# Low parts of the weights at another address remainder: residue 64 instead of 128 modulo 256

## The reference

```python
x = x + 0.5 * swiglu(rms_norm(x, ffn1_norm), w_gate, w_up, w_down)   # (silu(h @ w_gate) * (h @ w_up)) @ w_down
h = rms_norm(x, mix_norm)
z, xbc, dt, u = split(h @ w_in)
y_ssd  = ssd_group(z, xbc, dt, ...)        # conv, chunked scan over 16 heads, gate, grouped norm
y_pool = multiscale_pool_group(u, ...)     # trailing means over 2/4/8/16, a linear map per group
x = x + concat(y_ssd, y_pool) @ w_out
x = x + 0.5 * swiglu(rms_norm(x, ffn2_norm), w_gate2, w_up2, w_down2)
out = rms_norm(x, final_norm)
```

## The kernel before

| tensor | residue |
|---|---|
| `w_hi_part` (address 1152), `w_lo_part` (address 17536) | 128 |
| `xT`, `xghi`, `xglo` (lower four tiles of the normed input) | 128 |
| `xumhi`, `xumlo` (its upper four tiles in the mixer), `mixhi`, `mixlo`, `acthi`, `actlo` | 128 |
| `xufhi`, `xuflo` (its upper four tiles in the feed-forward blocks), `thi`, `tlo`, `post`, `gbuf` | 64 |

## Time and profile before

### The profile page before, as it was taken

The page is one execution under the profiler, slowest core; times in us unless marked ns, Lnnn a source line. Parts: engine busy times, 40 slices in busy tenths (PEclk is TensorE's granted clock), DMA queues, the critical chain, the costliest instruction groups (busy, mean ns, idle before and its releaser), DMA issues.

```text
span 999.2 us, 15359 instructions
## 1 busy us (share of the span) xinstructions
PE 984.2 (99%) x6118; PEld 867.7 (87%) x6118; DVE 781.2 (78%) x983; ACT 464.0 (46%) x603; POOL 215.8 (22%) x179
## 2 busy tenths in 40 slices
PE   9999999999999999999999999999999999999996
PEld 7799889998999868878787878889988999889975
DVE  5888478985698798786799886798956899568964
ACT  6655235552355556552224653545522555225532
POOL 1012002310022352321063461201300123002321
PEclk9999999999999999999999999999999999999998
DMA  9526304452232333323222232353551345313302
GB/s 264 151 61 161 104 22 127 127 148 85 60 108 67 103 108 94 97 64 83 66 85 66 67 101 85 87 146 86 145 149 45 85 124 153 106 42 105 107 22 85
DMA packets 188655, 99.63 MB, mean 100 GB/s; under 512 B 3524, under 2 KB 187944, under 8 KB 188584
## 3 DMA queue, kind: packets, MB, share of 16 engines
q1 hardware_dynamic: 187912, 97.60, 35.4%
q10 hardware_dynamic: 672, 1.05, 0.3%
HBM read 96.54 MB, written 2.10 MB: 99 GB/s over the span
## 4 chain that ended last, share of the span: by engine, by line
PE 91%; DVE 6%; issue 1%; ACT 1%; POOL 0%; POOLq 0%; DVEq 0%; ACTq 0%
PE bank L1643 12%; PE bank L1641 12%; PE bank L1642 12%; PE bank L1576 9%; PE bank L1578 9%; PE bank L1577 9%; PE bank L1659 8%; PE bank L1660 7%; PE bank L1661 7%; DVE w_lo_part L998 1%; PE bank L1730 1%; DVE actlo L1026 1%; PE bank L1724 1%; PE bank L1727 1%; DVE upd L1129 1%
## 5 line engine op out<-in xcount | busy, mean ns | idle before, releaser
L566 POOL TENSOR_TENSOR post<-post,rstd 128x256 f32<-128x256 f32 x57 | 93.1, 1634 | 520.9 <-DVE post L1088 520.9
L1641 PE MATMUL bank<-thi,w_hi_part 128*128 128x256 f32 x608 | 168.0, 276 | 0.0
L1642 PE MATMUL bank<-tlo,w_hi_part 128*128 128x256 f32 x608 | 167.9, 276 | 0.0
L1643 PE MATMUL bank<-thi,w_lo_part 128*128 128x256 f32 x608 | 167.9, 276 | 0.0
L998 DVE TENSOR_TENSOR w_lo_part<-w_raw,w_hi_part 128x1024 fp32r<-128x1024 f32 (+1 forms) x102 | 130.6, 1281 | 16.7 <-ACT w_hi_part L663 14.5
L1659 PE MATMUL bank<-acthi,w_hi_part 128*128 128x512 f32 x346 | 135.6, 392 | 2.1 <-DVE actlo L1026 2.1
L1661 PE MATMUL bank<-acthi,w_lo_part 128*128 128x512 f32 x346 | 134.7, 389 | 0.0
L1660 PE MATMUL bank<-actlo,w_hi_part 128*128 128x512 f32 x346 | 134.7, 389 | 0.0
L1641 PEld LDWEIGHTS bank<-thi,w_hi_part 128*128 128x128 f32 x608 | 114.2, 188 | 0.0
L1642 PEld LDWEIGHTS bank<-tlo,w_hi_part 128*128 128x128 f32 x608 | 114.2, 188 | 0.0
L1643 PEld LDWEIGHTS bank<-thi,w_lo_part 128*128 128x128 f32 x608 | 114.2, 188 | 0.0
(11 more groups left out here) (295 smaller groups left out, 2315.8 us busy)
## 6 DMA issues: line engine op xcount, KB each, us to landing
w_raw<-in_ffn_w_gate SPq DMA_DIRECT2D x42, 512.0 KB, 4.0
w_raw<-in_ffn_w_up SPq DMA_DIRECT2D x42, 512.0 KB, 5.2
w_raw<-in_ffn_w_down SPq DMA_DIRECT2D x32, 512.0 KB, 5.1
w_raw<-in_w_in SPq DMA_DIRECT2D x29, 512.0 KB, 3.8
w_raw<-in_w_out SPq DMA_DIRECT2D x16, 512.0 KB, 3.9
w_raw<-in_ffn_w_down SPq DMA_DIRECT2D x16, 384.0 KB, 4.4
out<-xtok SPq DMA_DIRECT2D x4, 512.0 KB, 3.1
xload<-in_x SPq DMA_DIRECT2D x3, 512.0 KB, 7.2
```

Of the source, the lines that this page charges most:

```text
L566: pool.tensor_tensor(gate, gate, rstd[:, half(h)], ALU.mult).then_inc(ready, 1)
L1641: pe.matmul(out, w, hi, start=opens and e == 0 and k == 0, stop=False, skip_group_check=True)
L1642: pe.matmul(out, w, lo, start=False, stop=False, skip_group_check=True)
L1643: mm = pe.matmul(out, wl, hi, start=False, stop=end, skip_group_check=True)
```

## The change

`w_lo_part` is moved up by 192 bytes: three small tables of 64 bytes each (`fold`, `a_exp`, `skip_row`) are declared between the two rings, and a fourth (`inv_count`, 64 bytes) behind `w_lo_part`, so that the next large tensor `xT` is 256 bytes higher than before and keeps its residue. The address of `w_lo_part` is 17728, its residue 64; `w_hi_part` stays at 1152. The tensors from `xT` to `par` are 256 bytes higher; what lies above the small tables stays where it was. The instructions of all engines, their order, their waits and the transfers are the same as before; lines from L223 on have another number (from the middle of the declarations on, one more).

```diff
         whi = sb("w_hi_part", [P, RING, UB, P], F32R)
+        fold = sb("fold", [2 * LOW, HEADS])
+        a_exp = sb("a_exp", [P, HEADS])
+        skip_row = sb("skip_row", [P, HEADS])
         wlo = sb("w_lo_part", [P, RING, UB, P], F32R)
+        inv_count = sb("inv_count", [P, PAD])
+        assert nc.sbuf_base % LANES == WEIGHT_LANE
         xT = sb("xT", [P, DK * S])
...
         eps = sb("eps", [P, 1])
-        inv_count = sb("inv_count", [P, PAD])
         dt_bias = sb("dt_bias", [2 * LOW, 1])
-        fold = sb("fold", [2 * LOW, HEADS])
-        a_exp = sb("a_exp", [P, HEADS])
-        skip_row = sb("skip_row", [P, HEADS])
         skip_col = sb("skip_col", [P, DK])
```

## The result

The changed kernel takes 1018.13 us (1017.57 to 1018.70, 2 runs) against 1001.16 before: the ratio is 1.017, with a 95% interval of 1.0146 to 1.0195. The forecast was 1006.5, with a range up to 1018.0. The span grew from 999.2 to 1015.8 us, by 16.6.

The account below looks back on a forecast made before the run. TensorE's matmul pace, start to start, was taken as the bound. Terms 6.1 + 0 − 0.5 − 0.3 = +5.3 us on 1000.9 gave 1006.2, forecast as 1006.5 us after 0.3 to the median; range 994 to 1018.

Parts of the forecast that it names:

- rival 2: Alternating differences inside every triple slow TensorE, half to all of 25 us: 1014 to 1026, taken as 1019; chance 0.16.
- the additive reading: Forecast's basis: each matmul's pace follows its own load-to-moving residue difference, alternation costing 0; 1002 to 1011 us, chance 0.42.
- (a): Second matmuls, 256 columns, moving residue 64: 912 now at equal residues, 113.3 to 120.0 ns, +6.1 us.
- (b): Second matmuls, 512 columns, moving residue 128: 746 with load 64 below, an unseen difference; taken as 0, ±4.5 us.
- (e): Cost of the difference alternating inside every triple: 0 to 25 us, 0.02 us per 256-column triple; taken as 0.
- Both signs: Named as proving the forecast wrong: the triples' other two matmuls carry the change, or the 512-column stages do.
- (c): Second matmuls, 256 columns, moving residue 128 (xglo): 152, between 0 and −1.0 us, taken as −0.5.
- (d): Second matmuls, 512 columns, moving residue 64: 48 go from 233 to 227 ns, −0.3 us.
- (f): VectorE's write of w_lo at residue 64 costs nothing more, nor do the moved small tables: 0.
- Rival 1: Only the moving operand's own residue counts, so nothing changes: 1001.2 us within 1 us; chance 0.20.
- Rival 3: Load 64 below the moving operand is faster: sum −5.8 us, 995.4 us, or 990 with two steps; chance 0.22.

Follow-up runs that it names:

- e3: Kernel before with both weight rings at residue 64 in place of 128, moving operands as before; 1020.4 us.
- e10: Changed kernel with grouped order in each unit: high times high and high times low for all blocks, then low times high; 1016.18 us, ratio 1.0146.
- e12: Kernel before with the lower tiles of xg (xghi, xglo) at residue 64 in the feed-forward blocks; 1009.22 us, ratio 1.0078.
- e1: Kernel before with all four small tables between the weight rings, low parts 256 bytes higher, residue still 128; 1001.19 us, ratio 1.0001.
- e6: Kernel before with both weight rings at residue 192 in place of 128, moving operands as before; 1026.0 us.
- e7: Kernel before with only the low weight parts moved, to residue 0, high parts still at 128; 1009.7 us.
- e13: e12 plus one 512-column matmul of xufhi (residue 64) ahead of each of four product groups behind down units; 999.28 us, ratio 0.9977.
- e15: As e13, but six added matmuls of 256 columns with acthi (residue 128) in place of the one; 1001.46 us.

## Why the prediction was wrong

The direction was right and the size was not: +5.3 us forecast, +17.0 measured, in the region of rival 2 (1014 to 1026), which had 0.16. The step that failed is the additive reading, by which each matmul feels its own load alone: it stands in (a) and in (b), and it is the reason for which (e) was set to 0. Both signs that the prediction had named for this came: the other two matmuls of the triples carry the change, and so do the 512-column stages.

- **(a)** gave the new difference a price in the second matmul of a triple, 6.7 ns, and left the other two alone: 6.1 us. Measured: all three matmuls at 117.8 ns, 353.4 per triple against 340, and 11.8 us for the same 912 triples. A difference in one of three places changes the pace of all.
- **(b)** was taken as 0 within ±4.5, and is the larger miss: the 512-column matmuls of down units and projections lost 7.8 us (4.2 + 1.7 + 1.1 + 0.8), of which shorter waits gave back at most 2.3. The reasoning that nothing faster than "equal" was seen held. But e3 gives the steady price of "64 below" as 228.8 − 226.7 = 2 ns in each matmul, and the changed kernel, with that difference in one of three, pays 4.1 in each on average. The excess goes with alternation: e10, which alternates less, has 227 in its high stretches and 228.5 on average over the down units.
- **(c)** −0.5 was −0.7. **(d)** −0.3 was −0.1 (`xuf` at 512 columns: 144 matmuls at 232.7 ns, where it was 233.4).
- **(e)** was the right term, set to 0. At 512 columns it is what happened, by e3 and e10. At 256 columns rival 2's picture, an unsettled triple each time, is not what happens: the stream settles. That it settles into the slower of e12's two patterns is read from the equal pace of 117.8 ns, and isn't shown beyond that. e10 keeps such a pace through eight matmuls without a switch. The 0.02 us per triple that I read from an entry was by chance near the 0.013 measured.
- **(f)** held: 1342 and 1341 ns; e1 shows that the tables cost nothing.
- Rival 1 and the Trainium skill's rule of independent ports (its page "TensorE: Matmul & The Clock Gate", section "What happens when you issue a matmul") gave no change; e3, e6 and the result disagree, with 120.0 against 113.3 ns for weights moved alone.
- Rival 3 said that a load 64 below is the good position: e3 has 228.8 there at 512 columns, not below 226.7.
- The 2%, or 20 us, that the prediction named as what a measurement can tell from no change was far too wide: the interval of the ratio is 0.25% to either side.

What stays open: what makes the two patterns, what else than the residues decides which one is entered (e6, e10), and why e7's residue 0 is harmless in the 256-column triples while 64 and 192 aren't. No run here resolves that, and only steps of 64 bytes were tried.

## What to carry to other kernels

Where TensorE is bound by the pace of fp32r matmuls, read that pace from start to start, for each kind of unit and each stretch, before and after any change of addresses. Prices of single matmuls don't add up: a change in one load of three moved all three, so bound such an edit by the slowest pattern seen times all matmuls, not by one step times those touched. And if one code at one set of addresses shows two paces, try another matmul at the way in: one of 0.23 us at each of four places gave back 9.9 us here, and with the lower tiles at 64 made the only version faster than the kernel before, by 0.2% (999.28 us). It was not tried on the kernel before by itself, whose product units but A11 run at 113.3 ns already.

## What the runs showed of the hardware

- The pace of a stream of fp32r load and matmul pairs depends on the address of the weights relative to the moving operand, modulo 256, tried in steps of 64 bytes (256 bytes more for the low parts change nothing, e1): 113.3 to 120.0 ns at 256 columns, 226.7 to 233.3 at 512, at a granted clock of 0.996 to 0.998.
- At 256 columns and weights 64 above, two patterns repeat themselves, with 113.3 and 117.8 ns on average (e12, and A11 in e6), and in e12 they last for whole groups. In e13 to e15 a stream behind 512 columns at equal residues falls into the slow one, behind 512 columns with the weights 64 above, or behind six of 256 at equal residues, into the fast one. It is no general rule: in e6 both paces come behind 512 columns with the weights 64 above.
- Equal residues are the best position of the four at 512 columns (226.7 ns), and at 256 none is slower (120.0; 128 away, in e6, is as slow in part).
- VectorE's fp32r write of 128x1024 took 1342 ns at residue 128 and 1341 ns at 64.
